# PEER layers: another pace of row fetches and dots, another order of group loads on SP's queue, and other tiles for the up rows

## What is computed

```python
def block(xb):                      # 128 tokens at a time
    q = (xb @ w_query).reshape(-1, PEER_HEADS, 2, PEER_DKEY // 2)
    sc = jnp.einsum('thpc,hpkc->thpk', q, sub_keys)
    s1, i1 = lax.top_k(sc[:, :, 0], PEER_TOPK)      # 8 heads, 16 of 128 keys
    s2, i2 = lax.top_k(sc[:, :, 1], PEER_TOPK)
    cand = (s1[..., :, None] + s2[..., None, :]).reshape(-1, PEER_HEADS, 256)
    top, ci = lax.top_k(cand, PEER_TOPK)
    idx = e1 * PEER_NKEYS + e2                      # one of 16384 experts
    g = jax.nn.softmax(top, axis=-1)
    hid = jax.nn.gelu(jnp.einsum('td,thkd->thk', xb, expert_down[idx]))
    return jnp.einsum('thk,thkd->td', g * hid, expert_up[idx])
```

## Time and profile before

| | |
|---|---|
| timed runs | median 3475.59 us of 3 (3459.72 to 3480.33) |
| profiled execution | 3480.13 us, span 3478.0 us |
| mean granted TensorE clock | 0.964 |
| TensorE matmuls | 3361.5 us busy (97%) |
| TensorE weight loads | 3050.2 us (88%) |
| VectorE | 1818.9 us (52%) |
| ScalarE | 1391.9 us (40%) |
| GpSimd | 1853.0 us (53%) |
| transfers | 808.21 MB, mean 232 GB/s |

### The profile page before, as it was taken

How to read it: one execution, slowest core, us unless ns; L and a number is a source line. 1 busy time by engine, 2 the same in 40 slices (tenths; PEclk the granted TensorE clock), 3 DMA queues, 4 the chain that set the end, 5 groups by cost and what they waited for, 6 DMA issues and landing times.

```text
span 3478.0 us, 47895 instructions
## 1 busy us (share of the span) xinstructions
PE 3361.5 (97%) x18808; PEld 3050.2 (88%) x18808; DVE 1818.9 (52%) x3788; ACT 1391.9 (40%) x2516; POOL 1853.0 (53%) x1071
## 2 busy tenths in 40 slices
PE   7998899999999899999999998999999999999999
PEld 6755789999999898899988887999999999889998
DVE  4525218995886444444422311699587744444443
ACT  3334223336786333333333322333477733333332
POOL 3400436776677545555544553477767773555553
PEclk9956899999999999999989998999999999999999
DMA  2200124667999888888732222366699998888884
GB/s 106 97 13 1 67 85 163 223 201 269 385 383 394 318 296 320 309 325 318 282 109 97 85 83 81 121 209 199 217 359 383 387 359 304 319 309 318 324 309 165
DMA packets 234302, 808.21 MB, mean 232 GB/s; under 512 B 21088, under 2 KB 70240, under 8 KB 225376
## 3 DMA queue, kind: packets, MB, share of 16 engines
q1 hardware_dynamic: 160352, 536.69, 43.4%
q0 software_dynamic: 73728, 268.47, 20.0%
HBM read 702.32 MB, written 102.76 MB: 231 GB/s over the span
## 4 chain that ended last, share of the span: by engine, by line
PE 84%; DMA 6%; ACT 4%; POOL 3%; DVE 2%; issue 2%; SPq 0%; DVEq 0%; ACTq 0%
PE banks L233 23%; PE banks L234 22%; PE banks L235 22%; PE banks L956 3%; PE banks L920 2%; DMA arena<-down,side 2%; ACT arena L783 2%; POOL weights_lo L213 2%; PE banks L491 2%; PE banks L480 1%; PE banks L248 1%; PE banks L249 1%; PE banks L250 1%; PE banks L280 1%; ACT weights_hi L207 1%
## 5 line engine op out<-in xcount | busy, mean ns | idle before, releaser
L213 POOL TENSOR_TENSOR weights_lo<-raw_ring,weights_hi 128x1024 fp32r<-128x1024 f32 x498 | 1273.0, 2558 | 1121.8 <-ACT weights_hi L207 1120.3
L233 PE MATMUL banks<-operand_hi,weights_hi 128*128 128x384 f32 (+1 forms) x4800 | 1676.5, 349 | 29.0 <-POOL weights_lo L213 14.7
L234 PE MATMUL banks<-operand_lo,weights_hi 128*128 128x384 f32 (+1 forms) x4800 | 1650.1, 344 | 0.0
L235 PE MATMUL banks<-operand_hi,weights_lo 128*128 128x384 f32 (+1 forms) x4800 | 1649.7, 344 | 0.0
L233 PEld LDWEIGHTS banks<-operand_hi,weights_hi 128*128 128x128 f32 x4800 | 906.9, 189 | 118.9 <-issue 73.3
L234 PEld LDWEIGHTS banks<-operand_lo,weights_hi 128*128 128x128 f32 x4800 | 906.9, 189 | 29.3 <-issue 3.6
L235 PEld LDWEIGHTS banks<-operand_hi,weights_lo 128*128 128x128 f32 x4800 | 906.0, 189 | 28.3
L207 ACT CAST weights_hi<-raw_ring 128x1024 fp32r<-128x1024 f32 x624 | 652.9, 1047 | 676.9 <-PE banks L235 580.0
L1121 DVE TENSOR_TENSOR residual<-residual,banks 128x384 f32<-128x384 f32 x256 | 141.9, 554 | 654.8 <-PE banks L235 645.3
L812 ACT ACTIVATE arena<-banks 128x384 f32<-128x384 f32 x256 | 126.0, 492 | 523.3 <-PE banks L235 472.4
L783 ACT ACTIVATE arena<-operand_hi,side 128x128 f32<-128x128 f32 x768 | 235.4, 393 | 51.3 <-DVE operand_hi L1085 46.6
(11 more groups left out here) (175 smaller groups left out, 2798.0 us busy)
## 6 DMA issues: line engine op xcount, KB each, us to landing
raw_ring<-weight_tiles SPq DMA_DIRECT2D x624, 512.0 KB
hid_scratch<-arena SPq DMA_DIRECT2D x64, 768.0 KB
gate_scratch<-arena SPq DMA_DIRECT2D x24, 2048.0 KB
arena<-hid_scratch SPq DMA_DIRECT2D x32, 1536.0 KB
arena<-gate_scratch SPq DMA_DIRECT2D x32, 1536.0 KB
arena<-up,side POOLq DMA_INDIRECT x146
residual<-x_t SPq DMA_DIRECT2D x2, 1024.0 KB, 6.7
arena<-key_t SPq DMA_DIRECT2D x2, 1024.0 KB, 5.1
```

The source lines that it names most:

```text
L213: eng.tensor_tensor(wl[:, b, :], raw[:, n % RING, :], wh[:, b, :].bitcast(F32), ALU.subtract).then_inc(done, 1)
L233: pe.matmul(out, w_hi, x_hi[:, c, :], start=start and c == 0, stop=False)
L234: pe.matmul(out, w_hi, x_lo[:, c, :], start=False, stop=False)
L235: last = pe.matmul(out, w_lo, x_hi[:, c, :], start=False, stop=stop and c == DC - 1)
```

## The change

It makes 42 dots during the routing of blocks 1 to 3 (17 places a block, a dot at most of them), 54 in the unit stage (nine for eight units), 6 behind the last unit, 6 more between the slices and the low halves of group 0, and 20 in up tiles 0 to 9, two a tile and ahead of all else of that tile; the gathers' tiles follow the dots. The turn moves from tile 67 to 70 and the units from 70 to 73. Gate group 1 is issued behind hidden group 1, hidden group 0 at tile 123, gate group 0 at tile 125. Quads run from up tile 18 to 114, 3.1 apart, weights are made from up tile 11 on, and the accumulator is copied, transposed and added in up tiles 116, 117 and 119.

```diff
-        UNIT_FROM = 70
+        UNIT_FROM = 73
         UNIT_TILE = [UNIT_FROM + u * 7 // 8 for u in range(UNITS)]
         TURN_TILE = UNIT_FROM - 3
-        EARLY_DOTS = 12
+        ROUTE_DOTS, UNIT_DOTS, TAIL_DOTS = 42, 54, 12
-        QUAD_TILE = [12 + q * 36 // 10 for q in range(QUADS)]
+        QUAD_TILE = [18 + q * 31 // 10 for q in range(QUADS)]
+        W_TILE = 11
...
-        GATHER_DOWN_AT = [17 + k for k in range(DOWN_RING)]
-        GATHER_DOWN_AT += [36 + (k - 6) % 4 + (k - 6) // 4 * 16 for k in range(6, 6 + EARLY_DOTS)]
-        GATHER_DOWN_AT += [UNIT_TILE[min((k - 18) // 2, UNITS - 1)] + 1 + max(0, (k - 18) // 2 - UNITS + 1)
-                           for k in range(6 + EARLY_DOTS, P)]
-        GATHER_UP_AT = [PDOWN - 3 + j for j in range(UP_RING)]
+        def dot_tile(k):
+            if k < ROUTE_DOTS:
+                return 19 + k * 51 // ROUTE_DOTS
+            k -= ROUTE_DOTS
+            if k < UNIT_DOTS:
+                return UNIT_TILE[k * UNITS // UNIT_DOTS]
+            k -= UNIT_DOTS
+            if k < TAIL_DOTS:
+                return UNIT_TILE[-1] + 1 + k
+            return PDOWN + (k - TAIL_DOTS) // 2
+
+        GATHER_DOWN_AT = [17 + k // 2 if k < DOWN_RING else dot_tile(k - DOWN_RING) + 1 for k in range(P)]
+        UP_ORDER = [6] + [(P - DOWN_RING + i) % DOWN_RING for i in range(DOWN_RING)]
+        GATHER_UP_AT = [PDOWN - 4] + [dot_tile(P - DOWN_RING + i) + 1 for i in range(DOWN_RING)]
...
-                if h == PDOWN - 7:
+                if h == UNIT_TILE[-1] + 9:
                     load_hid(0)
+                if h == UNIT_TILE[-1] + 11:
                     for half in range(2):
                         sp.wait_ge(s.gate_stored[half], was["gate_stored"] + 16 * (GATE_BLOCKS // 2))
                     load_gate(0)
-                    load_gate(1)
...
             load_hid(1)
+            load_gate(1)
...
-                if v == 0:
+                if v == W_TILE:
                     act.wait_ge(s.dotted, was["dotted"] + P)
                     act.activation(hid_g, hid_g, ACT.Gelu_apprx_tanh).then_inc(s.hid_g, 1)
-                if v == 8:
+                if v == W_TILE + 4:
                     act.wait_ge(s.w_turned, was["w_turned"] + 1)
...
-                if v == PUP - 3:
+                if v == QUAD_TILE[-1] + 2:
                     act.wait_ge(s.quads, was["quads"] + QUADS)
                     act.copy(pair[:, :, :], acc).then_inc(s.acc_copied, 1)
...
-                if j == 1:
-                    pool.wait_ge(s.dotted, was["dotted"] + P)
+                if 1 <= j < UP_RING:
+                    pool.wait_ge(s.dotted, was["dotted"] + P - DOWN_RING + j)
...
-                if v == PUP - 2:
+                if v == QUAD_TILE[-1] + 3:
                     pe.wait_ge(s.acc_copied, was["acc_copied"] + 1)
...
+            def dot_until(n):
+                while dots[0] < n:
+                    dot()
...
+            points = [0]
+            def route_dots():
+                points[0] += 1
+                dot_until(ROUTE_DOTS * points[0] // (3 * 17))
...
-                route(tt, dot)
+                route(tt, route_dots)
...
                 dve.tensor_tensor(oh1[:, u % 2], iota8, of_tokens(0, 8 * u), ALU.is_equal).then_inc(s.onehots, 1)
-                dot()
-                dot()
-            while dots[0] < P:
-                dot()
+                dot_until(ROUTE_DOTS + UNIT_DOTS * (u + 1) // UNITS)
+            dot_until(ROUTE_DOTS + UNIT_DOTS + TAIL_DOTS // 2)
...
             for j in range(GROUP):
                 gate_slice(0, j)
+            dot_until(ROUTE_DOTS + UNIT_DOTS + TAIL_DOTS)
             for j in range(GROUP):
                 gated_lo(0, j)
...
+                dot_until(min(P, ROUTE_DOTS + UNIT_DOTS + TAIL_DOTS + 2 * v + 2))
                 if v + AHEAD < PUP and LO_ON_DVE[u0 + v + AHEAD]:
                     split_lo(dve, u0 + v + AHEAD, lo_dve)
-                if v == 2:
+                if v == W_TILE + 1:
                     dve.wait_ge(s.hid_g, was["hid_g"] + 1)
                     dve.tensor_tensor(hid_g, hid_g, g_own, ALU.mult).then_inc(s.w_made, 1)
+                if v == QUAD_TILE[-1] + 5:
+                    for half in range(2):
+                        dve.wait_ge(s.acc_turned, was["acc_turned"] + half + 1)
...
-            for half in range(2):
-                dve.wait_ge(s.acc_turned, was["acc_turned"] + half + 1)
```

More of the change, by code:

```diff
@@ L871, in gather_up @@
                 t = row_token(j)
-                pool.indirect_dma_start(ring[(j + 6) % UP_RING], None, up_rows[layer],
+                pool.indirect_dma_start(ring[UP_ORDER[j % UP_RING]], None, up_rows[layer],
                                         bass.IndirectOffsetOnAxis(ap=experts_t[:, t:t + 1], axis=0)).then_inc(up_gathered[j % UP_RING], 16)
@@ L956, in rows_up @@
                         last = pe.matmul(acc[32 * g:32 * g + 32, d, :], zeroed[:, c % 2, z0:z0 + 32],
-                                         ring[(4 * q + g + 6) % UP_RING][:, d * 512:(d + 1) * 512],
+                                         ring[UP_ORDER[(4 * q + g) % UP_RING]][:, d * 512:(d + 1) * 512],
                                          start=False, stop=q == QUADS - 1, skip_group_check=True)
@@ L966, in peer_pe @@
                              ready=(lambda c, g=g: pe.wait_ge(s.gated_lo, was["gated_lo"] + 8 * g + c + 1)) if v % 8 == 0 else None)
-                if v == 5:
+                if v == W_TILE + 3:
                     pe.wait_ge(s.w_made, was["w_made"] + 1)
@@ L1009, in route @@
                 link(last)
+                between()
                 for hp in range(2 * PH):
@@ L1027, in route @@
                                        first_keys[:, :, 1, None, :].to_broadcast([P, PH, TOPK, TOPK]), ALU.add))
-                between()
                 ci3 = ci.rearrange("p (h k) -> p h k", h=PH)
@@ L1112, in peer_dve @@
                 g, k = v // 8, v % 8
+                dot_until(min(P, ROUTE_DOTS + UNIT_DOTS + TAIL_DOTS + 2 * v + 2))
                 if v + AHEAD < PUP and LO_ON_DVE[u0 + v + AHEAD]:
                     split_lo(dve, u0 + v + AHEAD, lo_dve)
-                if v == 2:
+                if v == W_TILE + 1:
                     dve.wait_ge(s.hid_g, was["hid_g"] + 1)
                     dve.tensor_tensor(hid_g, hid_g, g_own, ALU.mult).then_inc(s.w_made, 1)
+                if v == QUAD_TILE[-1] + 5:
+                    for half in range(2):
+                        dve.wait_ge(s.acc_turned, was["acc_turned"] + half + 1)
+                        dve.tensor_tensor(xt[:, 4 * half:4 * half + 4, 0:G], xt[:, 4 * half:4 * half + 4, 0:G],
+                                          ps[:, (7, 4)[half], :].rearrange("p (c t) -> p c t", c=4), ALU.add).then_inc(s.rows_added, 1)
                 if g + 1 < GROUPS:
@@ L1123, in peer_dve @@
                     gated_lo(g + 1, k)
-            for half in range(2):
-                dve.wait_ge(s.acc_turned, was["acc_turned"] + half + 1)
-                dve.tensor_tensor(xt[:, 4 * half:4 * half + 4, 0:G], xt[:, 4 * half:4 * half + 4, 0:G],
-                                  ps[:, (7, 4)[half], :].rearrange("p (c t) -> p c t", c=4), ALU.add).then_inc(s.rows_added, 1)
         sv = arena[:, 0:8192].rearrange("p (t v) -> p t v", t=TT)
```

4 lines of the change are left out of this document (3 added, 1 removed).

## The result

The changed kernel took 3485.32 us (median of 13 runs), the kernel before in the same runs 3469.48: ratio 1.0051, 95% interval 1.0031 to 1.0071. Forecast was 14 us faster; it came out some 16 slower. The profiled executions show only part of it: span 3478.0 before, 3483.8 after, 5.8 more. The one of the kernel before (3480.13) lies at the slow end of its runs, that of the changed kernel (3485.58) at its median.

What follows compares the result with a forecast made beforehand. TensorE's matmuls cover 97% of the span, so only its waits and lower clock can be gained. -17.2 + 24 + 21.5 - 20.6 + 6.4 = 14.1 us gained: 3466.0 profiled, 3461 us timed, range 3425 to 3495.

Steps and rivals of the forecast that it cites:

- Routing: Routing stretch: 42 dots where 12 were make VectorE finish late; cost 17.2 us, 8.6 a layer, bounds 0 and 16.
- tail: Tail of the down stage: spaced group loads and fewer rows let weight tiles come in time; gain 21.5 us, bounds 8 to 23.
- turn: Turn to the up stage: late gate group 1 and two dots delay up tile 3's low split; cost 20.6 us.
- units: Unit stage: 54 dots where 96 were remove waits for rows and clock loss; gain 24 us, bounds 10 to 28.
- ends: Ends of both layers: accumulator work and output stores move into the up tiles; gain 6.4 us, bounds 3 to 7.
- rival C: Unit stage keeps its waits, since ScalarE alone is the cause; 3485 us, chance 0.10.
- The first dot's wait: Routing of token block 1: VectorE stands 14.7 us for its first row, where it stood 7.2.
- routing itself: VectorE's routing work without dots and first wait, 164.3 us before, taken as the same after the change.
- The stand at the turn: End of routing, before the units: routing complete at 826.8, so TensorE stands 5.2 us, followed by a lower clock.
- the rule: Shared SBUF port pair: GpSimd cannot write descriptors while VectorE holds it; set aside because gather issues took 937 to 957 ns.
- rival B: Up tiles 1 to 9: VectorE becomes the bound and row waits reach TensorE; costs 56 us, 3517 us, chance 0.11.
- Rival A: Routing end and turn to the up stage: both new waits are covered; 3423 us, chance 0.22.

Runs made afterwards that it cites:

- e10: Changed kernel with its 42 routing dots all ahead of the index arithmetic's comparisons, multiplications and sums, none between them; ratio 0.9976 to the kernel before.
- e6: Changed kernel with 30 routing, 78 unit-stage and 20 tail dots, none in up tiles; median 3445.12 us, ratio 0.9909 to the kernel before.
- e9: Changed kernel with 30 routing, 86 unit-stage, 12 tail dots, none in up tiles, gate group 1 right behind gate group 0; median 3420.26 us, ratio 0.9861.
- e11: Changed kernel with all twelve tail dots ahead of the slices of group 0; ratio 1.0004 to the kernel before.
- e2: Changed kernel with gate group 1 issued right behind gate group 0, not behind hidden group 1; ratio 1.0026 to the kernel before.
- e3: Changed kernel with the 20 dots of the up tiles moved into the unit stage (74 there); ratio 0.9953 to the kernel before.
- e1: Kernel before with only the up rows' new tiles and the early accumulator ends; median 3460.87 us, ratio 0.9975.
- e12: e9 with the first seven up gathers one a tile from down tile 124 on; median 3416.48 us (4 runs), ratio 0.9850 to the kernel before.
- e8: Kernel before with only the changed order of group loads: gate group 0 two tiles behind hidden group 0, gate group 1 behind hidden group 1; ratio 1.0002.
- e7: Changed kernel with 30 routing, 78 unit-stage, 20 tail dots, none in up tiles, gate group 1 right behind gate group 0; ratio 0.9903 to the kernel before.

## Why the prediction was wrong

Its sign was wrong: 14.1 us of gain forecast, 5.8 lost in the profiled execution and some 16 between the medians. Routing, tail and turn were 15.3, 8.7 and 13.1 worse than worked out, units and ends 8.0 and 1.2 better: 27.9 in all, the whole distance from +14.1 to the -13.8 of the parts. (The blocks' small gaps and the unchanged stretches make the span 5.8 longer and not 13.8.) Routing is the largest miss, but not the only one: with routing as forecast the parts would sum to 1.5 gained, not 14.1. The median of 3485 is also what rival C gives; that is chance, since C's mechanism did not occur. And the forecast of 3461 started from a median of three runs, 3475.6; over 13 runs it is 3469.5.

**1. Routing: the step that failed.** The first dot's wait was right (14.96 against 14.7), and so was a dot's price of 1.15. Wrong was the term of 164.3 us, "routing itself", carried over as a constant. From the second point (589.5) to the end of the last dot (828.5) are 239.1; less 15.0 and 42 x 1.15 are 175.8, so 11.5 more. Comparisons, multiplications and the two small operations cost 12.5 more (55.3 against 42.8), another cast 1.2 less. The constant already held such waits: six multiplications at 4.37 us for 2.29 are 12.5 us of the 164.3. e10 shows that it is no price of 42 dots but of their places. The upper bound for this step (16 a layer, measured 17.2 and 15.3) named GpSimd's wait for a dot in one tile only, 69, ahead of the turn; the large stands are inside the stretch, where no dot place is for 8 us. The stand at the turn, forecast as 5.2, was 1.3, because TensorE had been held back before.

This is also where the rule was dismissed too soon. The row of 937 to 957 ns for a gather's issue is of down rows, mostly of the unit stage, where VectorE's long operations read PSUM. Of the 256 up gathers of the same trace 66 took over 1 us, up to 1.71, so "by the row no gather is held" did not hold even before the change. In the changed kernel single issues took up to 3.03 us, and the comparisons of the stretch 2.35 to 5.67. The up gathers before, the down gathers after:

```profile
L872 POOL DMA_INDIRECT arena<-up,side x146: 937/955/1702, 1167.8 to 3428.1; - x146
```

```profile
L870 POOL DMA_INDIRECT arena<-down,side x126: 937/955/3032, 603.2 to 2910.2; - x126
```

The Trainium skill (SBUF — State Buffer, "SBUF: two separate sides") says that the port pair is shared and the loser waits for the whole instruction: the trace agrees, with the cast of 2.10 us that ends with GpSimd's split. I had applied it to the up tiles and not to the routing, to which 30 more gathers a layer had just been moved beside the longest SBUF operations of the kernel.

**2. Units: right mechanism, gain larger** (32 for 24). I left 4.4 us and more for tiles with two units where ScalarE would be late; nothing of that was left. Rival C is out, and e6 and e9 show that 78 and 86 dots would have been as good.

**3. Tail: gain 12.8 instead of 21.5.** What was worked out held: the weight tile behind gate group 0 came in time. What was missed is a chain through three engines, slices, dot, gather, low split, worth 3.2 + 1.7 and 4.6 + 3.4. The step counted rows and bytes, and did not ask who waits for the six dots behind the slices. e11 removes it.

**4. Turn: cost 33.7 instead of 20.6.** The first stand was right: 10.7 and 10.0 for 2.9 + 7.3 and 3.9 + 7.3, since the slice came 13.0 us behind the issue of hidden group 1 where it had come 8.7 behind (1188.24, issue at 1179.55), and e2, without that load, has 5.7 and 6.6. Wrong was the term of 1.3 a layer for up tiles 3 to 10. Two waits for rows (2.06 and 1.78, at the two dots of up tile 4) made a second stand of 4.5 and 3.5, with 3.4 of clock of its own: 14.8 in both layers. That is rival B's mechanism in small, and e3 removes it; rival B at 56 us is out.

**5. Ends: right** (2.1 for 1.9, 5.5 for 4.5); e1 has them alone.

Rival A is out: both new waits were there. Open is how much of e10's gain comes from each half of its edit, and whether its places would add anything to e12.

## What to carry over

When work is moved beside another engine's, the moved work's own price is the easy term; the price of what stays can change too, so look at which long instructions share a memory side with it, and read a row for a clean price only in a stretch with the same neighbours. Even pace isn't the aim: put the work in the stretch that has slack by bytes and by engine (here 30, 86, 12 was the best tried), and never put an instruction that others wait for behind one that waits for a large load. Look at both sides of a turn when loads change their order: in e8 the order alone moved a wait across it, while in e2 the earlier load cost the tail nothing.

## What had not been expected

Two engines in step can double an instruction over a whole stretch: all six multiplications of the kernel before took 4.37 us, and five of the six comparisons of the changed kernel 4.5 to 5.7, where 2.29 is possible. The row was there to be read before the change: one operation at twice the time of another of the same shape, beside splits of 3.4 us that take 2.4 elsewhere. What a short stand costs in clock varies: those of 4.5 us were followed by 3.4 us lost at the lower level, those of 3.2 to 3.4 by 1.7 or by 3.4, that of 10.9 by 5.1, one of 2.2 (e10) by 1.7, while one of 1.8 us (e7) and one of 3.6 (e1, unit stage of layer 0) were followed by none.
